# A two-block transformer on one core: rounded features and their remainders in one 512-column matmul, two halves of a bank summed on VectorE

## The reference

```python
def rms_norm(x, gain):
    xf = x.astype(jnp.float32)
    y = xf * lax.rsqrt(jnp.mean(xf * xf, axis=-1, keepdims=True) + RMS_EPS)
    return (y * gain.astype(jnp.float32)).astype(x.dtype)
...
    for i in range(DEPTH):
        ...
        x = x + memory_cross_attention(rms_norm(x, norm_mem[i]), rms_norm(mem, norm_mem_src[i]), ...)
        x = x + swiglu(rms_norm(x, norm_ffn[i]), ffn_w_in[i], ffn_w_out[i])
```

## Time and profile before

| | us |
|---|---|
| median of 3 runs | 1661.8 |
| lowest and highest | 1661.35, 1661.95 |
| span of the profiled execution, first to last instruction | 1659.6 |
| TensorE busy | 1619.1 (98%) |
| VectorE busy | 1096.3 (66%) |
| ScalarE busy | 891.3 (54%) |
| GpSimd busy | 421.5 (25%) |

### The profile page before, as it was taken

One profiled execution on the slowest core, in us unless ns is written; L12 is line 12 of the kernel. 1 busy time (PEld: TensorE's weight loads), 2 busy tenths in 40 slices (PEclk: granted clock), 3 DMA queues, 4 the chain that ended last, 5 costly groups with the idle time before them and its releaser, 6 DMA issues. The chain is left out here.

```text
span 1659.6 us, 26949 instructions
## 1 busy us (share of the span) xinstructions
PE 1619.1 (98%) x10929; PEld 1462.8 (88%) x10929; DVE 1096.3 (66%) x1546; ACT 891.3 (54%) x1401; POOL 421.5 (25%) x460
## 2 busy tenths in 40 slices
PE   8999999999999999999999999999999999999999
PEld 7767899987887889998889998999888999999997
DVE  6875665645576665655577768777646876867763
ACT  6465554434455555443456746566445684756652
POOL 2500100002341120000147802244204690214430
PEclk9999999999999999999999999999999999999999
DMA  7523376556330236665555444766556444376652
GB/s 278 174 77 101 103 205 194 185 197 213 99 135 27 77 102 172 185 186 193 174 195 164 147 133 147 189 185 190 181 154 220 159 153 130 131 204 187 190 179 76
DMA packets 287067, 265.30 MB, mean 160 GB/s; under 512 B 12256, under 2 KB 247520, under 8 KB 286944
## 3 DMA queue, kind: packets, MB, share of 16 engines
q1 hardware_dynamic: 286944, 263.59, 50.8%
HBM read 262.52 MB, written 1.05 MB: 159 GB/s over the span
## 5 line engine op out<-in xcount | busy, mean ns | idle before, releaser
L144 DVE TENSOR_TENSOR w_lo<-w_raw,w_hi 128x2048 fp32r<-128x2048 f32 (+2 forms) x244 | 565.8, 2321 | 288.6 <-ACT w_hi L143 283.6
L143 ACT ACTIVATE w_hi<-w_raw 128x2048 fp32r<-128x2048 f32 (+2 forms) x244 | 462.9, 1902 | 214.6 <-PE bank L529 125.5
L1873 PE MATMUL bank<-h_hi,w_hi 128*128 128x256 f32 x1984 | 565.5, 285 | 4.7 <-issue 1.2
L1874 PE MATMUL bank<-h_lo,w_hi 128*128 128x256 f32 x1984 | 561.3, 283 | 0.0
L1875 PE MATMUL bank<-h_hi,w_lo 128*128 128x256 f32 x1984 | 561.2, 283 | 0.0
L1873 PEld LDWEIGHTS bank<-h_hi,w_hi 128*128 128x128 f32 x1984 | 380.5, 192 | 8.2 <-issue 7.5
L1874 PEld LDWEIGHTS bank<-h_lo,w_hi 128*128 128x128 f32 x1984 | 380.7, 192 | 0.1
L1875 PEld LDWEIGHTS bank<-h_hi,w_lo 128*128 128x128 f32 x1984 | 380.6, 192 | 0.0
L456 PE MATMUL bank<-w_hi,h_hi 128*128 128x512 f32 (+1 forms) x288 | 113.4, 394 | 5.4 <-DVE w_lo L144 3.3
L2953 POOL TENSOR_TENSOR cffn_hidden<-cffn_conv 128x256 f32<-128x256 f32 x44 | 73.7, 1675 | 155.5 <-ACT cffn_conv L2984 155.5
L457 PE MATMUL bank<-w_lo,h_hi 128*128 128x512 f32 (+1 forms) x288 | 111.9, 388 | 0.0
(11 more groups left out here) (447 smaller groups left out, 2858.0 us busy)
## 6 DMA issues: line engine op xcount, KB each, us to landing
w_raw<-in_w_in SPq DMA_DIRECT2D x48, 1024.0 KB, 5.0
w_raw<-in_ffn_w_in SPq DMA_DIRECT2D x88, 512.0 KB, 5.0
w_raw<-in_w_up SPq DMA_DIRECT2D x88, 512.0 KB, 5.2
w_raw<-in_ffn_w_out SPq DMA_DIRECT2D x22, 1024.0 KB, 4.9
w_raw<-in_w_down SPq DMA_DIRECT2D x22, 1024.0 KB, 5.0
w_raw<-in_nsa_w_in SPq DMA_DIRECT2D x10, 1024.0 KB, 5.2
w_raw<-in_mem_w_kv SPq DMA_DIRECT2D x8, 1024.0 KB, 5.1
w_raw<-in_w_branch SPq DMA_DIRECT2D x8, 1024.0 KB, 5.1
```

The source lines that it names most:

```text
L143: return act.activation(hi, raw, ACT.Copy)
L144: return dve.tensor_tensor(self.lo[:, cut_slot, 0:k * n], raw, hi.bitcast(F32), ALU.subtract)
L1873: pe.matmul(out, h, hi[:, f, :], start=(f == 0), stop=False)
L1874: pe.matmul(out, h, lo[:, f, :], start=False, stop=False)
```

## The change

Three edits. (1) `h_hi` and `h_lo` become two halves of one tile `h`. (2) In the feed-forward stage of the first block a new `summed_job` takes the place of `stationary_job`: for each weight tile one matmul of 512 columns streams a rounded feature tile and its remainder behind each other past the rounded weights, into a whole bank; a second matmul of 256 columns adds the product of weight remainder and rounded features to the bank's first half. A job has 32 matmuls and fills two banks, one for gate and one for up. (3) VectorE sums the two halves of each bank with a `tensor_reduce` over pairs that lie 256 columns apart, before it multiplies.

```diff
--- before.py
+++ after.py
@@ -45,6 +45,11 @@
 def heads(tensor, col, nh, dh, width):
 
     return free(tensor[:, :, :], [[width, T], [dh, nh], [1, dh]], col)
+
+
+def both(hi, lo):
+
+    return free(hi, [[lo.offset - hi.offset, 2], [1, hi.shape[-1]]])
 
 
 def row_bcast(dram, n, offset=0):
@@ -929,7 +934,8 @@
         self.mix_gain, self.ffn_gain = self.keep("mix_gain", [P, KD]), self.keep("ffn_gain", [P, KD])
         self.half_power = self.keep("half_power", [P, 1])
         self.row_stat = self.keep("row_stat", [P, 5, T])
-        self.h_hi, self.h_lo = self.keep("h_hi", [P, KD, S], F32R), self.keep("h_lo", [P, KD, S], F32R)
+        h = self.keep("h", [P, 2, KD, S], F32R)
+        self.h_hi, self.h_lo = h[:, 0, :, :], h[:, 1, :, :]
         self.tables = self.keep("rope_tables", [P, 2, 4, 8])
         self.raw = self.keep("w_raw", [P, Weights.RAW, Weights.SIZE])
         self.w_hi = self.keep("w_hi", [P, Weights.CUT, Weights.SIZE], F32R)
@@ -1707,7 +1713,8 @@
         h_hi, h_lo = k.h_hi, k.h_lo
         wide_hi, wide_lo = k.small("wide_hi", [P, KF, S], F32R), k.small("wide_lo", [P, KF, S], F32R)
         cols = k.gains_1[:, (1 + 4 * layer) * KD:(4 + 4 * layer) * KD]
-        gate, hidden = k.small("gate", [P, 2, S]), k.small("hidden", [P, 2, S])
+        gate, upper = k.small("gate", [P, 2, S]), k.small("upper", [P, 2, S])
+        hidden = k.small("hidden", [P, 2, S])
         k.attention_buffers()
         next_gain = s("next_gain")
         rows_q = Features(k, "rows_q", k.x, cols[:, 0:KD], h_hi, h_lo, k.norm_scratch, 4, first=4)
@@ -1723,6 +1730,7 @@
         down = Residual(k, "down", a["ffn_w_out"][layer], KF, wide_hi, wide_lo, bank=4, final=True, then=after,
                         factor=rows_f.rstd)
         opened, silu, prod, hid_hi, hid_lo = s("opened"), s("silu"), s("prod"), s("hid_hi"), s("hid_lo")
+        gate_done, gate_sum, up_sum = s("gate_done"), s("gate_sum"), s("up_sum")
 
         k.ready()
         with nc.Block() as block:
@@ -1813,17 +1821,27 @@
                 for j in range(KF + 1):
                     if j < KF:
                         w.cut_to(dve, up[j] + 2)
-                        dve.wait_ge(w.used, up[j] + 1)
+                        bank = k.bank[BANKS[2 * (j % 2)]]
+                        dve.wait_ge(gate_done, j + 1)
+                        if j >= 2:
+                            dve.wait_ge(prod, j - 1)
+                        dve.tensor_reduce(gate[:, j % 2, :], free(bank[:, :], [[1, S], [S, 2]]), AX.X, ALU.add).then_inc(gate_sum, 1)
+                    if j >= 1:
+                        i = j - 1
+                        bank = k.bank[BANKS[2 * (i % 2) + 1]]
+                        dve.wait_ge(w.used, up[i] + 1)
+                        dve.tensor_reduce(upper[:, i % 2, :], free(bank[:, :], [[1, S], [S, 2]]), AX.X, ALU.add).then_inc(up_sum, 1)
+                    if j < KF:
                         if j == 0:
                             dve.wait_ge(row_factors.done, 1)
-                        dve.tensor_tensor(gate[:, j % 2, :], k.bank[BANKS[j % 4]][:, 0:S], row_factors.rows, ALU.mult)\
-                           .then_inc(opened, 1)
+                        dve.wait_ge(gate_sum, j + 1)
+                        dve.tensor_tensor(gate[:, j % 2, :], gate[:, j % 2, :], row_factors.rows, ALU.mult).then_inc(opened, 1)
                     if j >= 1:
-                        i = j - 1
                         dve.wait_ge(silu, i + 1)
+                        dve.wait_ge(up_sum, i + 1)
                         if i >= 2:
                             dve.wait_ge(hid_lo, i - 1)
-                        dve.tensor_tensor(hidden[:, i % 2, :], k.bank[BANKS[i % 4]][:, S:2 * S], gate[:, i % 2, :], ALU.mult)\
+                        dve.tensor_tensor(hidden[:, i % 2, :], upper[:, i % 2, :], gate[:, i % 2, :], ALU.mult)\
                            .then_inc(prod, 1)
                     if j >= 2:
                         hid_rest(j - 2)
@@ -1850,7 +1868,8 @@
 
                 residual.pe(pe, part=part)
                 for j in range(KF):
-                    stationary_job(k, pe, up[j], k.bank[BANKS[j % 4]], rows_f, (prod, j - 3) if j >= 4 else None, j == 0)
+                    summed_job(k, pe, up[j], [k.bank[BANKS[2 * (j % 2) + tile]] for tile in range(2)], rows_f,
+                               ((gate_sum, j - 1), (up_sum, j - 1)) if j >= 2 else None, gate_done, j == 0)
                     if j == 0:
                         row_factors.pe(pe)
                 down.pe(pe, lambda pe, f: pe.wait_ge(hid_lo, f + 1))
@@ -1876,6 +1895,24 @@
         if tile == 0 and middle is not None:
             middle(pe)
     ins.then_inc(w.used, 1)
+
+
+def summed_job(k, pe, c, banks, features, free_banks, tile_done, first=False):
+
+    w, hi, lo = k.weights, features.hi, features.lo
+    w.wait_cut(pe, c)
+    whi, wlo = w.halves(c)
+    for tile in range(2):
+        if free_banks is not None:
+            pe.wait_ge(*free_banks[tile])
+        bank = banks[tile]
+        for f in range(KD):
+            if tile == 0 and first:
+                features.wait_feature(pe, f)
+            h, l = whi[:, f, tile * P:(tile + 1) * P], wlo[:, f, tile * P:(tile + 1) * P]
+            pe.matmul(bank[:, :], h, both(hi[:, f, :], lo[:, f, :]), start=(f == 0), stop=False)
+            ins = pe.matmul(bank[:, 0:S], l, hi[:, f, :], start=False, stop=(f == KD - 1))
+        ins.then_inc(tile_done if tile == 0 else w.used, 1)
 
 
 def block_nsa(k, a):
```

## The result

The changed kernel took 1693.99 us (median of 4 runs, 1692.86 to 1694.33) against 1661.57 us before: a ratio of 1.0195 with a 95% interval of 1.0181 to 1.0208. The forecast was 1693.3 us. The profiled execution has a span of 1691.1 us, 31.5 us more than before; it is the fastest of the four.

The account below looks back on a forecast made before the run. The closed chain of ScalarE and VectorE, 5.25 us per job, grows by 2 x 0.60 to 6.45, above TensorE's 5.55: 15.7 us per layer, 31.5 in all, span 1691.1, forecast 1693.3 us for timed runs, range 1671 to 1718.

Parts of the forecast that it names:

- The matmul term: On TensorE, a pair of tiles goes from 0.36 to 0.347 us, 9.4 us less over 704 pairs, not on the path.
- The sums: On VectorE between cut and gate product, two sums per job at 0.60 us each, priced by reductions of 512 elements.
- slow strided reads: Rival: sums reading columns 1 KB apart on VectorE cost double per element, 1.2 us each, 1742 us; chance 0.10.
- cheap sums: Rival: sums on VectorE occupy only 0.33 us each but stand in the chain, 1671 us; chance 0.05.
- The chain: ScalarE and VectorE steps without overlap in each feed-forward round grow from 5.25 to 6.45 us per job; chance 0.80.
- The buffers: Two jobs fill four banks, so TensorE's second half of job j waits for the up sum of job j - 2.
- The first wait: TensorE's second half of job 2 in layer 0 waits 3.4 us for the first up sum, until 217.45 us.
- The start: In layer 0, job 0 ends at about the old time and the first gate sum stands at 210.53 us.
- The end: After VectorE's last round in layer 0, the third down chunk is cut at 353.0 us, needed at 353.7.
- The cover: Time between the third down chunk's cut and TensorE's need of it shrinks from 4.5 to 0.7 us, just enough.
- The clock: Rival: pauses of some 0.9 us per job drop TensorE to 1.2 GHz, 10.7 us per job; chance 1 in 100.

Follow-up runs that it names:

- no sums: Changed kernel with both sums left out, gate and hidden products reading the first half of their banks: 1659.54 us, ratio 0.9993.
- sums first: Changed kernel with the cut moved behind both sums, so they stand ahead of it in VectorE's round: 1656.63 us, ratio 0.9974.
- adjacent: On top of sums first, the two halves of a feature tile lie side by side, read as one contiguous piece: 1657.20 us, ratio 0.9976.
- narrow matmuls: Changed kernel with each 512-column matmul taken apart into two of 256 columns: 1693.51 us, ratio 1.0195.
- three pairs: Changed kernel with three pairs of banks in turn, two for the last four jobs: 1695.15 us, ratio 1.0206.
- up sum late: Changed kernel with the up sum moved behind the gate product: 1705.36 us, ratio 1.0269.
- no up sum: Changed kernel with the up sum left out, the hidden product reading the first half of the up bank: 1678.63 us, ratio 1.0108.

## Why the prediction was right

*The matmul term* was mis-sized, and did not matter. It took 0.3467 us per pair from the two spacings of the earlier trace rows, 9.4 us in all. Measured on kernels in which TensorE sets the pace, a pair takes 0.3533 us in five of the six stages traced (no sums, sums first, adjacent) and 0.3465 in one, so the edit is worth 4.7 us with both stages at the first level or 9.5 with both at the second, and was 4.2 us in the median of sums first. As the prediction said, the term is off the path of the changed kernel (narrow matmuls). TensorE: Matmul & The Clock Gate (Trainium skill), section "Back-to-back issue gap", gives N/2.4 + 2.5 ns for an isolated warm matmul, by which, as an estimate, the term would be 1.8 us. The two stages lie 4.4 us (adjacent, 2 x 2.2) and 6.7 us (sums first) below those of before, so the traces do not agree with that price for this stream.

*The sums.* 0.60 us each in the queue was right to the digit, and so was the choice of row: same operation, same memory, same elements read. Pairs 1 KB apart cost nothing extra, and 256 results cost no more than two. The rivals of slow strided reads and of cheap sums are ruled out by these rows. SBUF — State Buffer (Trainium skill), section "Door 1: The DMA port swizzle", speaks of matmuls on a PSUM pattern that is not contiguous; the 0.68 us of both kinds of reduction show no such effect on VectorE, and no run here tested it for matmuls.

*The chain* of 6.45 us was right, and the experiments show it as a chain: take a sum out and the period falls by the sum less the wait it covered (0.60 - 0.19 = 0.41 us), put it behind the gate product and the period grows, put both into the idle time ahead of the cut and the cost is gone.

*The buffers.* The first wait (3.4 us forecast) is 3.20 us from the last start to the next, less a normal 0.12, so 3.1 us. That this wait sets the time was never claimed, and three pairs confirms that it does not.

*The start.* The first gate sum came 10.78 us after the first up matmul, forecast 10.84; the absolute 209.98 against 210.53 is a stage that began 0.49 us earlier in this execution. *The end.* The third down chunk's cut began at 350.37 and took 2.3 us, so it was there at 352.66, 10.2 us after the first down matmul, and TensorE took its first matmul 10.92 us after:

```profile
350.37 2.29 DVE L149 TENSOR_TENSOR w_lo<-w_raw,w_hi 128x2048 fp32r<-128x2048 f32 x1 [1.38 <-ACT w_hi L148]
...
353.37 0.39 PE L530 MATMUL bank<-w_hi,mf_wide_hi 128*128 128x512 f32 x1
```

The cover was 0.7 us, as calculated, and held.

*The clock* fell once per layer, at the end of the longest wait; the rival, given 1 in 100, was a fall in each job, and that did not come. The row it was weighed by, the first 41 us, had shown that a share of idle time is harmless, but not one idle stretch of 3 us. That the fall cost nothing was not foreseen; it lay in an early round, and three pairs shows the same fall in a late one costing 0.4 to 0.7 us per layer. The prediction had no row at the lower level, but the trace of before holds one, in another stage: TensorE, busy for 2.38 of the 3.80 us ahead of it, had a granted clock of 0.50 from 423.9 to 427.2 us.

## What to carry to other kernels

Find the closed chain before pricing an addition: if the period of two engines that hand work to each other equals the sum of the steps, an instruction costs its full time, less any wait that it covers, anywhere inside, however idle both engines look. In the stretch where one waits for the other it costs nothing, as long as it fits (here 1.20 us into 1.95). When a stage starts late and catches up, its early rounds show the chain's own period and so its slack (here 0.51 us of 5.76, against two sums of 0.60). The same change with its two sums written ahead of the cut is 0.26% faster than the kernel before instead of 1.95% slower.

## What the runs showed of the hardware

- A stream that alternates 512- and 256-column matmuls, each with its own weights, settles at 0.3533 or 0.3465 us per pair and, where TensorE never waited, kept its level to the end of the stage, some 20 jobs; a stream of 256 columns kept 0.120 us and one of 512 columns 0.227 us. The level changed between two layers of one execution of one kernel and across a wait (0.347 us in the half job before the first wait and 0.353 once the clock was back, in layer 0 of the changed kernel). Whether the operand is contiguous did not decide it. What does is open.
- After 2.8 to 3.9 us of standing still in these stages (changed kernel, up sum late, no up sum, three pairs, in both layers) TensorE worked for a few microseconds at 1.2 GHz (a pair in 0.64 us); the fall began between 0.7 us before and 1.3 us after it started again; after waits of 0.5 us, and after the one of 1.4 us in no sums (pairs 0.367 us on average in the half job behind it, in either layer), the clock did not fall. In narrow matmuls the same wait, 2.65 us in layer 0 and 2.66 us in layer 1, was followed by a granted clock of 1.00 in the first and 0.66 in the second over the 5 us behind it, so the length of the wait alone does not decide.
- An instruction of VectorE that needs the result of the one just before it starts 0.72 to 0.79 us after the start of a 512-element sum instead of 0.60: the wait costs 0.12 to 0.19 us, and another instruction in between hides it (up sum late: 0.72 and 0.78; no up sum: 0.79; changed kernel, with the up sum in between: 0.60 each).
